# Causal mask of two attentions: added by VectorE in PSUM instead of by TensorE's identity matmul

## The reference, cut to what matters

```python
# NSA, selected and window branch, one block of queries
s = jnp.einsum('bqghd,bgqkd->bghqk', qb, ks).astype(f32)
p = masked_softmax(s, valid)             # valid: key position <= query position
o_slc = jnp.einsum('bghqk,bgqkd->bqghd', p.astype(dtype), vs)
...
# differential attention, one block of queries
causal = key_pos[None, :] <= qpos[:, None]
def probs(qb, k):
    sc = jnp.einsum("bqhd,bkhd->bhqk", qb, k,
                    preferred_element_type=jnp.float32) * scale
    return jax.nn.softmax(jnp.where(causal, sc, NEG_INF), axis=-1)
w = probs(qb1, k1) - lam * probs(qb2, k2)
```

## Time and profile before

| | us |
|---|---|
| median of 3 runs | 2066.51 |
| lowest, highest | 2066.39, 2069.49 |
| span of the profiled execution, first to last instruction | 2065.7 |
| PE busy | 2030.8 (98%) |
| DVE busy | 1301.5 (63%) |
| ACT busy | 974.8 (47%) |
| NSA stage, 424 to 806: PE busy | 380.12 of 382.00 |
| first half of differential attention, 1006 to 1072: PE busy | 65.74 of 66.00 |

### The profile page before, as it was taken

The page is one execution under the profiler, slowest core; times in us unless marked ns, Lnnn a source line. Parts: engine busy times, 40 slices in busy tenths (PEclk is TensorE's granted clock), DMA queues, the critical chain, the costliest instruction groups (busy, mean ns, idle before and its releaser), DMA issues.

```text
span 2065.7 us, 31956 instructions
## 1 busy us (share of the span) xinstructions
PE 2030.8 (98%) x12513; PEld 1788.3 (87%) x12513; DVE 1301.5 (63%) x1770; ACT 974.8 (47%) x1414; POOL 83.7 (4%) x84
## 2 busy tenths in 40 slices
PE   8999999999999999999999999999999999999998
PEld 7898898888989898889899898888888888888886
DVE  6799776456666666658666666556546555655655
ACT  5554554344444444446445546544434434434443
POOL 2000042000000000100000001000000000000000
PEclk9999999999999999999999999999999999999999
DMA  8245576545455554755554554666666666566663
GB/s 284 93 138 188 172 213 216 171 133 173 142 160 148 154 162 133 244 169 170 161 166 152 160 155 149 200 184 191 193 189 191 191 194 185 189 196 186 189 196 105
DMA packets 202935, 360.87 MB, mean 175 GB/s; under 512 B 25360, under 2 KB 33904, under 8 KB 202160
## 3 DMA queue, kind: packets, MB, share of 16 engines
q1 hardware_dynamic: 200656, 351.88, 55.3%
q0 software_dynamic: 1664, 5.97, 0.9%
q10 hardware_dynamic: 480, 1.10, 0.1%
HBM read 356.03 MB, written 2.10 MB: 173 GB/s over the span
## 4 chain that ended last, share of the span: by engine, by line
PE 90%; DVE 6%; ACT 2%; issue 2%; DMA 0%; ACTq 0%; POOL 0%; DVEq 0%; POOLq 0%
PE acc L517 35%; PE acc L521 19%; PE banks L517 8%; PE banks L1113 6%; PE acc L1113 6%; PE banks L1116 3%; PE acc L1116 3%; DVE w_high_low L1764 1%; PE acc L607 1%; ACT w_high_low L1157 1%; PE banks L882 1%; PE acc L548 1%; PE banks L910 1%; PE banks L999 1%; PE banks L977 1%
## 5 line engine op out<-in xcount | busy, mean ns | idle before, releaser
L1764 DVE TENSOR_TENSOR w_high_low<-raw,w_high_low 128x1024 fp32r<-128x1024 f32 x648 | 795.1, 1235 | 611.1 <-ACT w_high_low L1157 609.8
L1157 ACT ACTIVATE w_high_low<-raw 128x1024 fp32r<-128x1024 f32 x648 | 682.0, 1059 | 735.6 <-PE acc L517 329.7
L521 PE MATMUL acc<-x_high_low,w_high_low 128*128 128x256 f32 x3648 | 454.7, 285 | 0.7 <-issue 0.7
L521 PEld LDWEIGHTS acc<-x_high_low,w_high_low 128*128 128x128 f32 x3648 | 443.9, 192 | 3.5 <-issue 2.2
L517 PE MATMUL acc<-w_high_low,x_high_low 128*128 128x512 f32 x1728 | 413.9, 396 | 1.1 <-DVE w_high_low L1764 1.1
L517 PEld LDWEIGHTS acc<-w_high_low,x_high_low 128*128 128x128 f32 x1728 | 322.1, 188 | 68.2 <-issue 1.8
L517 PE MATMUL acc<-w_high_low,h_high 128*128 128x512 f32 x1088 | 292.6, 391 | 3.0 <-DVE w_high_low L1764 1.1
L517 PEld LDWEIGHTS acc<-w_high_low,h_high 128*128 128x128 f32 x1088 | 202.7, 188 | 45.9 <-issue 2.1
L517 PE MATMUL acc<-w_high_low,h_low 128*128 128x512 f32 x544 | 167.6, 389 | 0.0
L1113 PE MATMUL acc<-x_high_low,w_high_low 128*128 128x512 f32 x512 | 161.3, 396 | 1.5 <-DVE x_rows L2117 1.1
L1113 PE MATMUL banks<-x_high_low,w_high_low 128*128 128x512 f32 x512 | 160.8, 395 | 0.0
(11 more groups left out here) (362 smaller groups left out, 1635.7 us busy)
## 6 DMA issues: line engine op xcount, KB each, us to landing
raw<-in_b_w_in SPq DMA_DIRECT2D x128, 512.0 KB, 3.8
raw<-in_w_mlp_in SPq DMA_DIRECT2D x128, 512.0 KB, 3.7
raw<-in_w_mlp_out SPq DMA_DIRECT2D x128, 512.0 KB, 4.5
raw<-in_w_in SPq DMA_DIRECT2D x96, 512.0 KB, 4.0
raw<-in_kv_w SPq DMA_DIRECT2D x48, 512.0 KB, 4.1
raw<-in_a_w_in SPq DMA_DIRECT2D x32, 512.0 KB, 6.3
raw<-in_b_w_out SPq DMA_DIRECT2D x32, 512.0 KB, 4.7
raw<-in_w_out SPq DMA_DIRECT2D x32, 512.0 KB, 4.6
```

The source lines that it names most:

```text
L521: ins_ = nc.tensor.matmul(ACC[pair][:, m // 2, (m % 2) * TOK:(m % 2 + 1) * TOK], wa[:, k, j, m * P:(m + 1) * P], xa[:, kt + j, :], start=f ...
L1157: nc.scalar.activation(WH[:, s % SPLIT, :, :], RAW[:, s, :, :], ACT.Copy).then_inc(hi_ready, SLOTS + 1 if first_one else 1)
L1764: V.tensor_tensor(WL[:, k, :, :], RAW[:, p % SLOTS, :, :], WH[:, k, :, :].bitcast(F32), ALU.subtract).then_inc(lo_ready, SLOTS + 1 if isin ...
```

## The change

PE's mask matmul is taken out of both score functions, and the first score product of a bank now starts it. DVE adds the mask to the two diagonal blocks of the bank in one instruction of 2 x 128 elements per partition, from PSUM and the constants into PSUM, before the maxima. In NSA the maxima wait for that add (`steps.link`). In differential attention the adds of both banks come first, then one wait, then the four maxima. The rounded table and its cast are gone, and the group's count of steps grows by eight.

```diff
-GROUP_STEPS, QUARTER_STEPS = 55, 8
+GROUP_STEPS, QUARTER_STEPS = 63, 8
...
-    CAUSAL_R = at("causal_rounded", [P, 3 * P], F32R, placed["constants"] + 4 * _CONST["causal"][0])
...
                     h, keys = (n - 2) % 4, KS if n < 6 else KW
-                    nc.tensor.matmul(bank[:, 0:3 * P], ID_R[:, :], CAUSAL_R[:, :], start=True, stop=False, skip_group_check=True)
                     for t in range(NT):
...
-                                                start=False, stop=t == NT - 1, skip_group_check=True)
+                                                start=t == 0, stop=t == NT - 1, skip_group_check=True)
...
             for m in range(2):
-                nc.tensor.matmul(BK[m][:, 0:3 * P], ID_R[:, :], CAUSAL_R[:, :], start=True, stop=False, skip_group_check=True)
                 for t in range(NT):
...
-                                            start=False, stop=t == NT - 1, skip_group_check=True)
+                                            start=t == 0, stop=t == NT - 1, skip_group_check=True)
...
+        def diagonal(x):
+            return x.rearrange("p (b q) -> p b q", b=3)[:, 0:3:2, :]
+
+        def causal(bank):
+
+            d = diagonal(bank[:, 0:3 * P])
+            return V.tensor_tensor(d, d, diagonal(const("causal")), ALU.add)
+
...
-                steps.inc(V.tensor_copy(CAUSAL_R[:, :], const("causal")))
                 steps.inc(V.tensor_copy(ID_R[:, :], const("ident")))
...
+                steps.link(causal(BK[n % 2]))
                 for t in range(NT):
                     lo, w = (0, P) if t == 0 else (P, TOK)
                     ins_ = V.tensor_reduce(NM[:, n % 2, t:t + 1], BK[n % 2][:, lo:lo + w], AX_X, ALU.max, negate=True)
...
                     if i == 4 * h:
                         for m in range(2):
                             v.wait_ge(a_full, 2 * n + m + 1)
+                            steps.inc(causal(BK[m]))
+                        steps.wait()
+                        for m in range(2):
                             for t in range(NT):
```

More of the change, by code:

```diff
@@ L2490, in head_split @@
             split(HH[:, kt, :], HL[:, kt, :], TMP[:, order % 2, 0, :])
-        def diagonal(x):
-            return x.rearrange("p (b q) -> p b q", b=3)[:, 0:3:2, :]
         def second_stage(kind, j, i):
```

## The result

The changed kernel takes **2080.4 us** (median of 4 runs, 2079.6 to 2083.7) against 2067.8 us for the kernel before, timed beside it. The ratio is 1.0064, 95% interval 1.0051 to 1.0076: slower by 13 us, between 10.5 and 15.7. The forecast was slower by 8.2 us, and the time lies 0.9 us above its range.

A forecast was written before the change was run, and what follows sets the result against it. PE, 98% busy, was taken to bound the kernel before, and the DVE and ACT loop NSA after the change. NSA +6.1, differential +2.4 and cast -0.26 summed to +8.2 us, 2074.7 us, range 2067.9 to 2079.5.

The forecast's parts named there:

- step 3: NSA: DVE's add lengthens its loop with ACT to 4.67 us per head, past PE's 4.33; +6.1 us over four groups.
- steps 1 and 4: PE: 48 mask matmuls worth 12.3 us if it stays the bound; differential heads: PE waits for later head rows, +2.4 us.
- Step 2: DVE: each of 48 adds takes 0.43 us plus 0.04 for the linked wait, 0.47 us; between 0.34 and 0.57.
- rival of the cheap link: DVE: the add overlaps its neighbour and takes 0.34 us; +3.0 us, 2069.5 us; chance 0.09.
- PE idle for ACT's exponentials before most turns, some 0.3 each: Expected sign in NSA: PE waits some 0.3 us before most turns from about the fourth on.
- rival in which no matmul's time is freed: PE: the matmuls go, but weight loads or the format change fill their time; +11.4 us, 2077.9 us; chance 0.04.
- Step 5: Start of the chain: the removed cast of the mask table saves its time there, -0.26 us.
- faster rival: NSA and differential turns: the longer loop is absorbed and PE keeps its whole saving; -12.6 us, 2053.9 us; chance 0.10.

The follow-up runs named there:

- after_both: Changed kernel with DVE's weight low part moved behind the maxima in NSA and the previous head's rows right behind the maxima in differential heads: 2061.6 us, ratio 0.9965.
- after: The changed kernel as first measured and profiled, mask added by DVE instead of PE: 2080.4 us, ratio 1.0064 against the kernel before.
- again: The changed kernel run once more, unedited: 2081.0 us, ratio 1.0060 against the kernel before.
- no_mask: Changed kernel with the causal mask of both attentions left out, neither PE's matmuls nor DVE's adds: 2062.0 us, ratio 0.9968.
- after_low: Changed kernel with DVE's 1.2 us low part of a weight slot moved behind the maxima in NSA: 2068.5 us, ratio 0.9994.
- nsa_twice: Changed kernel with DVE's mask add done twice in the NSA heads: 2093.7 us, ratio 1.0123.
- before_low: Kernel before, mask still on PE, with DVE's low part of a weight slot moved behind the maxima in NSA: 2066.8 us, ratio 0.9985.
- nsa_add: Changed kernel with the DVE add in NSA only; differential heads keep PE's mask matmul, rounded table and cast stay: 2078.3 us, ratio 1.0041.
- before_delay: Kernel before, mask on PE, with two idle DVE reductions ahead of the first z epilogue of each NSA group: 2078.7 us, ratio 1.0055.
- after_three: Changed kernel with DVE's low part, the previous head's rows and each NSA group's first z epilogue (slot 8 to 12) moved: 2058.3 us, ratio 0.9945.
- before_both: Kernel before, mask on PE, with DVE's low part and the previous head's rows moved behind the maxima: 2064.9 us, ratio 0.9984.

## Where the prediction was right, and which steps failed

The direction and its mechanism were right: the adds turn DVE, ACT and PE into one loop that PE waits for, and PE's saving is not in the sum. It was 4.3 us short of the 12.5 in the profiled execution: 1.4 for the clock, 1.3 in the differential heads and 1.7 ahead of NSA (+1.5 by the chance of the start, where -0.26 was forecast), less 0.1 in NSA. Two steps failed: step 3 put the TensorE clock at nothing, and steps 1 and 4 mis-sized what the mask matmuls free. By its own steps:

- **Step 2, the add.** 424 ns and 0.03 to 0.04 us for the link; 0.45 to 0.46 us a step against 0.47. The two unlinked adds of a differential head took 0.76 us in `after_both`; the linked ones overlap nothing. The linked step doubles at full price (0.89 us for two), so the rival of the cheap link is out. The sentence of the Trainium skill that stood beside it (VectorE: DVE Perf Modes, "The DRAIN you can't avoid": the semaphore costs nothing extra) does not agree with the traces: two adds take 0.76 us unlinked and 0.89 us linked. The 392 ns estimated from the errata table of the same page were 32 ns low.
- **Step 3, NSA.** +6.1 forecast, 5.9 by trace without the clock. The size is right, and not by luck: from the first add of a group to its eighth maxima the sum has 36.36 us, and DVE needs 36.30 (550.09 to 586.39 in its timeline). All 32 adds count. The place was not: the wait was expected at the turn, while most of it came at the values, behind the outputs that stand behind the z epilogue. "PE idle for ACT's exponentials before most turns, some 0.3 each" came to at most 0.2 us, shown by PE's weight loads and not by PE itself.
- **What step 3 lacked: the clock.** The sum had no term for it. Behind PE's two waits at a group's end it brings 1.1 to 1.4 us more, once in the traced execution of after, four times in that of `again`. That is the largest miss of the mechanism, 1.4 and 5.4 us. Without the 1.4 us the 2080.4 would be about 2079.0, inside the range.
- **Steps 1 and 4, the differential heads.** +2.4 forecast, +3.7 measured. The failed step is the price of the second mask matmul, 0.36 us from its start to the start of the scores, of which 0.19 are the end of the scores in front of it. With 0.35 in place of 0.54 us a head, head 0 gives -0.35 instead of -0.54 and heads 1 and 3 cost 0.64 instead of 0.45; head 2 keeps its 0.82. That makes 1.75 a half; the trace has 1.83, with -0.36 in head 0, 0.6 to 0.7 in heads 1 and 3 and 0.80 to 0.85 in head 2. The rival in which no matmul's time is freed was a third right there. NSA's 0.25 us a matmul is really 0.17, but nothing in the sum hung on it.
- **Step 5, the cast.** At the first group nothing of it is left in the profile after; both traces have a stretch at the lower clock near 100 us, not at the same instructions, and so cannot be compared there. In traces without that stretch it can be read: from 85 to 320 us the four without the cast (no_mask, after_low, after_both, nsa_twice) gain 1.31 to 1.37 us on the trace of before, the three with it (before_low, nsa_add, before_delay) 1.05 to 1.10. That is 0.2 to 0.3 us for the cast, as forecast.
- **The range.** It was built from the price of an add and from the rivals alone, and the two stages' own uncertainty was left at nothing, with no room for a start that differs by up to 4 us between executions, or for the clock.

PE as the bound, the faster rival, did not come. But `after_three` shows that its ground was real: with three of DVE's steps in other places the same adds give 2058.3 us, and between `before_both` and `after_three`, in neither of which a head makes PE wait, the mask's move is worth -8 us by the ratios (-8.9 by trace). The kernel before with all three steps moved was not run; in the trace of `before_both` PE has no wait in NSA that the third move could take away.

## What to carry to other kernels

Before work is moved from the busiest engine to one with idle time, list what the second engine does between two hand-overs to the first, and ask which of it must be there. Here the same 48 adds cost 13 us, or saved 8 against `before_both`, by whether a 1.2 us step, a 2.7 us step and one copy stood ahead of a hand-over or behind it. Price a removed instruction by the distance between its neighbours that stay, in a place where it is already missing, and not by the distance to its successor, which may still hold the end of the instruction in front of it. And where a change adds waits to the TensorE, put a term for its clock into the sum, with its own range.

## What the runs showed of the hardware

- A wait of PE is paid twice when the clock falls behind it: twelve products of 512 columns took 4.61 us in place of 3.10, at a granted clock of 0.53 and 0.62. The same program had one such stretch in an execution of 2080.0 us and four in one of 2083.8 us.
- A DVE add of 256 elements from PSUM and SBUF into PSUM takes 424 ns (430 in `after_low`), as the multiplication in SBUF does (425 ns).
- The start of a mask or gemm matmul behind fp32 scores is recorded 0.03 us behind the start of the last of them, and that one's own 0.22 us then stands in the distance to the next instruction: 0.36 us from the second mask matmul to its scores, 0.31 from a gemm's first matmul to its second, where it is 0.12 between later ones.
